# Output projections with both memory parts first, and two k-blocks of the gate ahead of the first head's odd scores

## The chip, the cores and the metric

One Trainium2 chip, one core of it. The time is the device time in microseconds of one execution. Three runs of the kernel before gave 2028.35, 2029.74 and 2031.55 us; the median is 2029.74 us.

## The reference, cut to what matters

The kernel computes a decoder trunk of two layers on a sequence of 512 tokens with 1024 channels. Layer 0 mixes with gated linear attention (GLA), layer 1 with a convolution module. In both, four memory heads attend to 256 memory rows, and one output projection takes the mixer's result `y` (1024 rows of the weight) and the memory heads' result `m` (512 rows) together.

```python
for i in range(2):
    x = layer_norm(ALPHA * x + 0.5 * swiglu(x, ffn1_w_gu[i], ffn1_w_down[i]), ...)
    if i == 0:
        y, qm = gla_mix(x @ gla_w_in, gla_w_gate2, gla_b_gate, gla_g_onorm)   # 4 heads, chunks of 64
        w_out = gla_w_out                                                     # (1024 + 512, 1024)
    else:
        y, qm = conv_mix(x @ conv_w_in, conv_w_dw, ...)
        w_out = conv_w_out                                                    # (1024 + 512, 1024)
    m = mem_attention(qm, mem, mem_w_kv[i])                                   # softmax over 256 rows
    x = layer_norm(ALPHA * x + concatenate([y, m]) @ w_out, ...)              # the projection changed here
    x = layer_norm(ALPHA * x + 0.5 * swiglu(x, ffn2_w_gu[i], ffn2_w_down[i]), ...)
```

In `gla_mix` the scores inside a chunk are `where(causal, qe @ ke^T, 0)`, and the result is multiplied by `silu(r)`, where `r` is a projection of `x` (the gate's projection below).

## The kernel before, in words

Activations are held with the channel on the partitions: eight blocks of 128 channels, each 128 x 512 (tokens). Every f32 product is made of three matmuls on rounded halves: high weight by high input, high weight by low input, low weight by high input (`mm3`, lines 1868 to 1870, for 512 tokens; `mm3_half`, lines 1879 to 1881, for one half of 256 tokens). ScalarE rounds a weight block to its high half (`whi`, line 715), VectorE (line 1180) or GpSimd (`lo_blocks`, line 539) makes the low half (`wlo`); `lo_ready` counts finished low halves. The order on each engine is written out by hand, engine by engine, and engines meet only at semaphores. TensorE runs its instructions in the order of its block.

**The output projection** works on pairs of output blocks: pairs 0 and 1 (blocks 0 to 3) for all 512 tokens, and the last two pairs (blocks 4 to 7) for each half of the tokens in turn. `out_a` (line 2123) multiplies the memory part, 4 k-blocks (`A_K`), `out_b` (line 2133) the mixer's part, 8 k-blocks (`B_K`), into the banks `OUT_BANKS`: pair 0 uses banks 0 and 1, pair 1 banks 2 and 3. `out_halves` (line 2150) then does blocks 4 to 7 and uses banks 0, 1 for its p = 0 and banks 2, 3 for its p = 1. For one half and one p, the memory part is 24 matmuls of 256 columns, the mixer's part (B) 48. The memory part's weights lie in a spare buffer (`a_spare`; its low halves are made by GpSimd in `spare_lo_parts`).

VectorE takes the banks away in `residual_out` (line 1427): `residual_pair` scales the layer's input (`scaled_x`, lines 1312 to 1317), adds the bank (line 1335, which increments `y_evac`), adds to the running sum (line 1291 or 1288) and to the running sum of squares (line 1299), whose squares ScalarE makes (line 779). Between pair 0 and pair 1 it makes the low half of one weight block (`split_lo(n0 + 6, 0)`, line 1180). The halves are taken away by `half_block` (line 1356), and after the first half the layer norm's sums are taken (`sums` on TensorE, lines 1929 and 1938). `y_evac` at `Y_BASE + 2` says that banks 0 and 1 are free again, at `Y_BASE + 4` that banks 2 and 3 are.

**The gated linear attention** runs head by head. `keys_and_att(h)` (line 2390) transposes the keys (line 2396), makes the scores of even sub-chunks (line 2402) in bank 5 and of odd ones (line 2408, "odd scores") in bank 6. Banks 6 and 7 held the transposed probabilities of the memory attention, which ScalarE (line 915) and VectorE (line 1568) copy out; so for head 0 the odd scores wait for `pt_evac`. `gates_of_r(first, count)` (line 2332) is the gate's projection, one k-block for two output blocks at a time (6 matmuls of 512 columns); its pieces are spread among the attention's steps. `outputs(0, 3)` (line 2210) makes the memory output of the fourth memory head. VectorE's `mask_att(0)` (line 1692) reads the scores when `att_mm` is incremented, and `state_sums` (line 2418) waits for it.

Of the kernel before, what the change touches and what calls it, by code (L numbers as in the profile page):

```python
# [102 lines left out]
def before(counts):  # L103
    return [sum(counts[:i]) for i in range(len(counts))]


Y_BASE = before(HALVED)
# [10 lines left out]
def half_no(ln, h, d):  # L118
    return HALF_BASE[ln] + (DK - HALVED[ln]) * h + d - HALVED[ln]
# [33 lines left out]
def build(nc, a, out):  # L153
# [3 lines left out]
    with ExitStack() as ctx:  # L157
        def sem(name):
            return ctx.enter_context(nc.semaphore(name))
# [9 lines left out]
        def sb(name, shape, dt=F32):  # L169
# [41 lines left out]
            ("ex0_hi", [P, 3, 4, P], F32R), ("ex0_lo", [P, 3, 4, P], F32R),  # L211
            ("t_hi", [P, 4, 4, HALF], F32R), ("t_lo", [P, 4, 4, HALF], F32R), ("hid", [P, FK, SEQ], F32))
        *_, s12_1 = views(("h_hi_7", [P, FK, SEQ], F32R), ("h_7", [P, FK - 2, SEQ], F32), ("s12_1", [P, 2, 4, P], F32))
        *_, p5_copy = views(("h_hi_8", [P, FK, SEQ], F32R), ("h_8", [P, FK, SEQ], F32), ("p5_copy", [P, HALF], F32))
        qkv, mo_hi_g, mo_lo_g, qm_g, bk, ke, v_tok = views(
# [57 lines left out]
        def a_spare(ln):  # L273

            return a_spare_g if ln == LN_GLA_OUT else a_spare_c

        def mean_at(ln):
# [9 lines left out]
        hi_ready, lo_ready, w_used = sem("hi_ready"), sem("lo_ready"), sem("w_used")  # L287
# [6 lines left out]
        y_even, y_evac, res_done, u0_ready, u_acc, q_acc, sq_done = (  # L294
            sem(n) for n in ("y_even", "y_evac", "res_done", "u0_ready", "u_acc", "q_acc", "sq_done"))
# [1568 lines left out]
        def _(pe):  # L1864
# [7 lines left out]
            def mm3(to, s, k, t, hi, lo, start, stop):  # L1872

                return mm3_of(to, whi[:, s], wlo[:, s], k, t, hi, lo, start, stop)

            def mm3_half(h, to, w_hi, w_lo, k, t, hi, lo, k_in, start, stop):

                w, tok = slice(t * P, t * P + P), slice(HALF * h, HALF * h + HALF)
                nc.tensor.matmul(to[:, tok], w_hi[:, k, w], hi[:, k_in, tok], start=start, stop=False, skip_group_check=True)  # L1879
                nc.tensor.matmul(to[:, tok], w_hi[:, k, w], lo[:, k_in, tok], start=False, stop=False, skip_group_check=True)  # L1880
                return nc.tensor.matmul(to[:, tok], w_lo[:, k, w], hi[:, k_in, tok], start=False, stop=stop,  # L1881
                                        skip_group_check=True)
# [38 lines left out]
            def sums(ln, h, spread=True):  # L1921

                tok, bs, no = tokens(ln, h), blocks(ln, h), half_no(ln, h, DK - 1) + 1
                if HALVED[ln] == DK:
                    pe.wait_ge(u_acc, ACC_BASE[ln] + DK - 1)
                else:
                    pe.wait_ge(u_half, no)
                if spread:
                    nc.tensor.matmul(mean_at(ln), ones[:, :], usum[:, tok], start=True, stop=True,
                                     skip_group_check=True).then_inc(mean_mm, 1)  # L1930
                for j, x in enumerate((usum, qsum)):
                    if j and HALVED[ln] == DK:
                        pe.wait_ge(q_acc, ACC_BASE[ln] + DK - 1)
                    elif j:
                        pe.wait_ge(q_half, no)
                    for b in bs:
                        c = 2 * bs[0] + len(bs) * j + b - bs[0]
                        last = nc.tensor.matmul(bank[5][:, c:c + 1], x[:, b * P:(b + 1) * P], ones[:, 0:1],
                                                start=(HALVED[ln] == DK and c == 0), stop=(j == 1 and b == bs[-1]),
                                                skip_group_check=True)  # L1940
                last.then_inc(stats_mm, 1)

            def spread_rstd(ln, h):

                tok = tokens(ln, h)
                pe.wait_ge(rstd_diag, UNIT[ln] + h + 1)
                nc.tensor.matmul(bank[7][:, tok], ones[:, :], diag_rstd[:, tok], start=True, stop=True,
                                 skip_group_check=True).then_inc(rstd_mm, 1)
# [201 lines left out]
            def out_halves(ln, n0, mo_hi, mo_lo, y_h, y_l):  # L2150

                spare = a_spare(ln)
                for h in range(2):
                    for p in range(2):
                        def memory_part(t):
                            for k in range(A_K):
                                mm3_half(h, bank[OUT_BANKS[2][h][2 * p + t]], spare[:, 0, A_K * p:A_K * p + A_K],
                                         spare[:, 1, A_K * p:A_K * p + A_K], k, t, mo_hi, mo_lo, k, h == 0 and k == 0, False)

                        if h == 0:  # L2160
                            pe.wait_ge(lo_ready, n0 + 5 + p)
                            pe.wait_ge(y_evac, Y_BASE[ln] + 2 * p + 2)
                            memory_part(0)
                            memory_part(1)
                            pe.wait_ge(lo_ready, n0 + 7 + p)
                        else:
                            pe.wait_ge(y_half, half_no(ln, 0, 5 + 2 * p) + 1)
                        for t in range(2):
                            to = bank[OUT_BANKS[2][h][2 * p + t]]
                            if h:  # L2170
                                memory_part(t)
                            for k in range(B_K):
                                last = mm3_half(h, to, whi[:, p], wlo[:, p], k, t, y_h, y_l, k, False, k == B_K - 1)
                            if h == 0 or t == 0:
                                last.then_inc(y_even, 1)
                            else:
                                last.then_inc(w_used, 1 if p else 3)
                            if h == 1 and p == 0:
                                if t == 0:
                                    sums(ln, 0)  # L2180
                                else:
                                    spread_rstd(ln, 0)
# [123 lines left out]
            n0 = GLA_N  # L2306
# [25 lines left out]
            def gates_of_r(first, count):  # L2332

                for i in range(first, first + count):
                    j, k = divmod(i, DK)
                    if k == 0:
                        pe.wait_ge(lo_ready, n0 + 12 + j + 1)
                        if j < 3:
                            pe.wait_ge(gla_evac, 21 + 2 * j)
                        else:  # L2340
                            pe.wait_ge(o_read, 16)
                    for t in range(2):
                        last = mm3(bank[R_BANK[j][t]][:, :], j % 2, k, t, xhi[:, k, :], xlo[:, k, :], k == 0, k == DK - 1)
                    if k == DK - 1:
                        last.then_inc(w_used, 1)
# [44 lines left out]
            def keys_and_att(h):  # L2390
                pe.wait_ge(prods, 4 * h + 4)
                pe.wait_ge(q_block, 2 * h + 2)
                if h:
                    pe.wait_ge(kdt_evac, h)
                for b in range(TB):
                    last = nc.tensor.transpose(bank[4][:, b * P:(b + 1) * P], qkv[:, 4 + h, b * P:(b + 1) * P], ident[:, :])
                last.then_inc(kdt_mm, 1)
                if h:
                    pe.wait_ge(att_evac, 2 * h)
                for b in range(TB):  # L2400
                    tok = slice(b * P, (b + 1) * P)
                    nc.tensor.matmul(bank[5][:, tok], ke[:, h, tok], qkv[:, h, tok], start=True, stop=True)
                if h:
                    pe.wait_ge(state_done, (TB - 1) * (h - 1) + 1)
                else:
                    pe.wait_ge(pt_evac, 2 * HEADS)
                for b in range(TB):
                    last = nc.tensor.matmul(bank[6][:, HALF + b * CHUNK:HALF + (b + 1) * CHUNK], ke[:, h, b * P:(b + 1) * P],
                                            q_odd[:, h, b, :], start=True, stop=True)
                last.then_inc(att_mm, 1)  # L2410

            def state_sums(h):
# [7 lines left out]
                last.then_inc(ds_mm, 1)  # L2420

            keys_and_att(0)
            gates_of_r(0, 2)
            outputs(0, 3)
            gates_of_r(2, 2)
            pe.wait_ge(mo_done, 4)
# [44 lines left out]
            n0 = CONV_N  # L2471
# [61 lines left out]
            ln = LN_FFN[3]  # L2533
# [59 lines left out]
```

## Time and profile before

| what | value |
|---|---|
| median of three runs | 2029.74 us |
| the profiled execution | 2030.78 us |
| its span, first to last instruction | 2028.9 us |
| TensorE busy | 2009.3 us, 99% |
| VectorE busy | 1349.0 us, 66% |
| ScalarE busy | 810.9 us, 40% |
| GpSimd busy | 816.9 us, 40% |
| mean granted clock of TensorE | 0.997 of full speed |

Times in the rows are microseconds from the span's start. PE is TensorE, DVE VectorE, ACT ScalarE, POOL GpSimd. A matmul's duration in the timeline includes its way through the array, so consecutive starts tell the pace: 256-column matmuls start 0.12 us apart, 512-column ones 0.23 us apart. "[1.82 <-DVE u L1335]" behind a row says that the engine was idle 1.82 us before it, and which instruction ended the idle time.

### The profile page before, as it was taken

How to read it: one execution, taken by the hardware profiler on the slowest of the kernel's cores; microseconds unless marked ns; L12 is line 12 of the kernel's file. 1: busy time of each engine (PE TensorE's matmuls, PEld its weight loads, DVE VectorE, ACT ScalarE, POOL GpSimd, SP SyncE). 2: the span in 40 equal slices, each digit the busy share in tenths (PEclk: the TensorE clock that was granted, in tenths of full speed). 3: DMA queues.
4: the chain of work that ended last, by engine and by line, in shares of the span. 5: the costliest groups of instructions: out<-in, count | busy, mean ns of one | idle time of the engine just before them, and what ended most of it. 6: DMA issues, size and time to landing. Idle time of an engine off the chain costs nothing.

```text
span 2028.9 us, 33888 instructions
## 1 busy us (share of the span) xinstructions
PE 2009.3 (99%) x13253; PEld 1841.2 (91%) x13253; DVE 1349.0 (66%) x1851; ACT 810.9 (40%) x1165; POOL 816.9 (40%) x575
## 2 busy tenths in 40 slices
PE   9999999999999999999999999999999999999998
PEld 9899998888988999999899999889887799999887
DVE  4477774553425768887466777646899986777645
ACT  5433352263433354444234444423353435433422
POOL 1588830044423458880015888001100435887000
PEclk9999999999999999999999999999999999999999
DMA  7533332332212235453232545323544322332232
GB/s 253 208 125 124 124 130 97 107 106 63 84 32 73 94 104 163 147 165 107 93 103 94 166 145 168 103 96 101 185 125 177 99 89 84 104 103 93 90 102 89
DMA packets 229511, 239.10 MB, mean 118 GB/s; under 512 B 5999, under 2 KB 222189, under 8 KB 227628
## 3 DMA queue, kind: packets, MB, share of 16 engines
q1 hardware_dynamic: 228780, 235.68, 35.4%
q10 hardware_dynamic: 640, 2.16, 0.3%
q8 instruction: 62, 1.02, 0.2%
q14 instruction: 29, 0.24, 0.0%
HBM read 215.80 MB, written 22.02 MB: 117 GB/s over the span
## 4 chain that ended last, share of the span: by engine, by line
PE 89%; DVE 3%; POOL 3%; ACT 2%; issue 2%; DMA 1%; DVEq 0%; SPq 0%; ACTq 0%; POOLq 0%
PE bank L1868 12%; PE bank L1869 12%; PE bank L1870 12%; PE bank L2004 11%; PE bank L2006 11%; PE bank L2005 11%; PE bank L1879 3%; PE bank L1880 3%; PE bank L1881 3%; PE bank L1958 1%; ACT whi L715 1%; DVE wlo L1180 1%; PE bank L1963 1%; PE bank L2327 1%; PE bank L2328 1%
## 5 line engine op out<-in xcount | busy, mean ns | idle before, releaser
L715 ACT CAST whi<-raw 128x2048 fp32r<-128x2048 f32 (+3 forms) x190 | 322.3, 1696 | 869.5 <-POOL scratch L599 433.9
L1180 DVE TENSOR_TENSOR wlo<-raw,whi 128x2048 fp32r<-128x2048 f32 (+2 forms) x164 | 355.1, 2165 | 232.8 <-ACT whi L715 232.6
L576 POOL TENSOR_TENSOR tiny<-tiny 128x2 f32<-128x2 f32 (+1 forms) x13 | 9.4, 725 | 567.1 <-DVE tiny L1460 567.1
L539 POOL TENSOR_TENSOR wlo<-raw,whi 128x256 fp32r<-128x256 f32 x128 | 100.2, 818 | 304.1 <-DVE wlo L1180 177.0
L595 POOL TENSOR_TENSOR raw<-raw 128x512 f32<-128x512 f32 x72 | 219.2, 3045 | 0.0
L1868 PE MATMUL bank<-h_hi,whi 128*128 128x512 f32 x528 | 207.1, 392 | 0.0
L1869 PE MATMUL bank<-h_lo,whi 128*128 128x512 f32 x528 | 205.5, 389 | 0.0
L1870 PE MATMUL bank<-h_hi,wlo 128*128 128x512 f32 x528 | 205.5, 389 | 0.0
L599 POOL TENSOR_TENSOR scratch<-raw,s 128x512 f32<-128x512 f32 x72 | 152.8, 2122 | 51.2 <-DVE ex_lo L1187 51.2
L2004 PE MATMUL bank<-t_hi,whi 128*128 128x256 f32 x576 | 163.7, 284 | 1.6 <-DVE bank L1247 1.6
L2004 PE MATMUL bank<-t_hi,ex_hi 128*128 128x256 f32 x576 | 163.8, 284 | 0.9 <-DVE bank L1239 0.4
L2005 PE MATMUL bank<-xlo,whi 128*128 128x256 f32 x576 | 163.1, 283 | 0.0
L2006 PE MATMUL bank<-xhi,wlo 128*128 128x256 f32 x576 | 163.1, 283 | 0.0
L2004 PE MATMUL bank<-xhi,whi 128*128 128x256 f32 x576 | 163.0, 283 | 0.0
L2005 PE MATMUL bank<-t_lo,whi 128*128 128x256 f32 x576 | 163.0, 283 | 0.0
L2006 PE MATMUL bank<-t_hi,wlo 128*128 128x256 f32 x576 | 163.0, 283 | 0.0
L2005 PE MATMUL bank<-t_lo,ex_hi 128*128 128x256 f32 x576 | 163.0, 283 | 0.0
L2006 PE MATMUL bank<-t_hi,ex_lo 128*128 128x256 f32 x576 | 163.0, 283 | 0.0
L1868 PE MATMUL bank<-xhi,whi 128*128 128x512 f32 x400 | 160.8, 402 | 0.0
L1869 PE MATMUL bank<-xlo,whi 128*128 128x512 f32 x400 | 157.2, 393 | 0.0
L1870 PE MATMUL bank<-xhi,wlo 128*128 128x512 f32 x400 | 157.0, 392 | 0.0
L592 POOL TENSOR_TENSOR s<-raw 128x512 f32<-128x512 f32 x72 | 97.4, 1353 | 128.4 <-DMA raw<-in_ffn_w_gu_dram 72.9
(376 smaller groups left out, 5808.5 us busy)
## 6 DMA issues: line engine op xcount, KB each, us to landing
raw<-in_ffn_w_gu_dram SPq DMA_DIRECT2D x88, 1024.0 KB, 4.9
raw<-in_ffn_w_down_dram SPq DMA_DIRECT2D x32, 896.0 KB, 4.6
raw<-in_ffn_w_down_dram SPq DMA_DIRECT2D x32, 512.0 KB, 3.4
raw<-in_gla_w_in_dram SPq DMA_DIRECT2D x14, 1024.0 KB, 5.0
early_raw<-in_conv_w_in_dram SPq DMA_DIRECT2D x18, 512.0 KB, 4.2
lo_scratch<-early_lo SPq DMA_DIRECT2D x18, 512.0 KB, 3.2
diag_scratch<-diag_tmp SPq DMA_DIRECT2D x8, 1024.0 KB, 7.9
raw<-in_conv_w_in_dram SPq DMA_DIRECT2D x16, 512.0 KB, 5.0
```

The lines of the kernel that those rows point to most:

```text
L539: last = nc.gpsimd.tensor_tensor(to[:, k, :], whole[:, k, :], high[:, k, :].bitcast(F32), ALU.subtract)
L592: nc.gpsimd.tensor_tensor(s12[s][:, 0], a21, a22, ALU.add).then_inc(w_sum, 1)
L595: nc.gpsimd.tensor_tensor(a21, a21, a11, ALU.add).then_inc(w_sum, 1)
L599: nc.gpsimd.tensor_tensor(s4, a12, s12[s][:, 1], ALU.add).then_inc(w_sum, 1)
L715: nc.scalar.copy(whi[:, s, 0:kc, 0:width], raw[:, s, 0:kc, 0:width]).then_inc(hi_ready, 1)
L1180: nc.vector.tensor_tensor(wlo[:, s, 0:kc, 0:width], raw[:, s, 0:kc, 0:width], whi[:, s, 0:kc, 0:width].bitcast(F32), ALU.subtract).then_in ...
L1868: nc.tensor.matmul(to, w_hi[:, k, w], hi, start=start, stop=False)
L1869: nc.tensor.matmul(to, w_hi[:, k, w], lo, start=False, stop=False)
L1870: return nc.tensor.matmul(to, w_lo[:, k, w], hi, start=False, stop=stop)
L2004: nc.tensor.matmul(to, w_hi[:, k], hi[:, k], start=(start and k == 0), stop=False, skip_group_check=True)
L2005: nc.tensor.matmul(to, w_hi[:, k], lo[:, k], start=False, stop=False, skip_group_check=True)
L2006: last = nc.tensor.matmul(to, w_lo[:, k], hi[:, k], start=False, stop=(k == 3), skip_group_check=True)
```

## The change

In `out_halves`, in the first token half, TensorE now does the memory parts of p = 0 and of p = 1 one after the other, each behind its own two waits, and then the mixer's parts (B) of p = 0 and p = 1. Before, it did memory and B of p = 0, then memory and B of p = 1. The second token half keeps its order. This holds for both layers' projections. In the GLA attention, the first two k-blocks of the gate's projection, which followed `keys_and_att(0)`, are now issued inside it, ahead of the wait for `pt_evac` and of the odd scores of head 0. No matmul is added or removed.

```diff
--- before.py
+++ after.py
@@ -2152,23 +2152,24 @@
                 spare = a_spare(ln)
                 for h in range(2):
                     for p in range(2):
-                        def memory_part(t):
+                        def memory_part(p, t):
                             for k in range(A_K):
                                 mm3_half(h, bank[OUT_BANKS[2][h][2 * p + t]], spare[:, 0, A_K * p:A_K * p + A_K],
                                          spare[:, 1, A_K * p:A_K * p + A_K], k, t, mo_hi, mo_lo, k, h == 0 and k == 0, False)
 
                         if h == 0:
-                            pe.wait_ge(lo_ready, n0 + 5 + p)
-                            pe.wait_ge(y_evac, Y_BASE[ln] + 2 * p + 2)
-                            memory_part(0)
-                            memory_part(1)
+                            for ahead in range(2 if p == 0 else 0):
+                                pe.wait_ge(lo_ready, n0 + 5 + ahead)
+                                pe.wait_ge(y_evac, Y_BASE[ln] + 2 * ahead + 2)
+                                memory_part(ahead, 0)
+                                memory_part(ahead, 1)
                             pe.wait_ge(lo_ready, n0 + 7 + p)
                         else:
                             pe.wait_ge(y_half, half_no(ln, 0, 5 + 2 * p) + 1)
                         for t in range(2):
                             to = bank[OUT_BANKS[2][h][2 * p + t]]
                             if h:
-                                memory_part(t)
+                                memory_part(p, t)
                             for k in range(B_K):
                                 last = mm3_half(h, to, whi[:, p], wlo[:, p], k, t, y_h, y_l, k, False, k == B_K - 1)
                             if h == 0 or t == 0:
@@ -2403,6 +2404,7 @@
                 if h:
                     pe.wait_ge(state_done, (TB - 1) * (h - 1) + 1)
                 else:
+                    gates_of_r(0, 2)
                     pe.wait_ge(pt_evac, 2 * HEADS)
                 for b in range(TB):
                     last = nc.tensor.matmul(bank[6][:, HALF + b * CHUNK:HALF + (b + 1) * CHUNK], ke[:, h, b * P:(b + 1) * P],
@@ -2420,7 +2422,6 @@
                 last.then_inc(ds_mm, 1)
 
             keys_and_att(0)
-            gates_of_r(0, 2)
             outputs(0, 3)
             gates_of_r(2, 2)
             pe.wait_ge(mo_done, 4)
```

## Rows read from the trace of the kernel before

**Rows 1.** The page, part 1: busy us (share of the span) x instructions.

```profile
PE 2009.3 (99%) x13253; PEld 1841.2 (91%) x13253; DVE 1349.0 (66%) x1851; ACT 810.9 (40%) x1165; POOL 816.9 (40%) x575
```

**Rows 2.** Waits of TensorE over the whole span: line <- released by: us in total, times, longest us.

```profile
PE bank L1879 <- DVE u L1335: 3.0, 2, 1.8
...
PE bank L2408 <- ACT u L915: 1.2, 1, 1.2
```

**Rows 3.** Timeline of TensorE, GLA projection: start us, us, engine, line, out<-in, forms, [idle].

```profile
671.77 0.32 PE L1879 MATMUL bank<-y_hi,whi 128*128 128x256 f32 x1
...
677.45 0.28 PE L1881 MATMUL bank<-y_hi,wlo 128*128 128x256 f32 x1
679.55 0.36 PE L1879 MATMUL bank<-mo_hi_g,a_spare_g 128*128 128x256 f32 x1 [1.82 <-DVE u L1335]
```

**Rows 4.** Timeline of VectorE in the same stretch.

```profile
669.37 2.29 DVE L1180 TENSOR_TENSOR wlo<-raw,whi 128x2048 fp32r<-128x2048 f32 x1
...
677.58 1.10 DVE L1317 SCALAR_TENSOR_TENSOR u<-xhi,u 128x512 f32<-128x512 f32 x1
678.71 0.69 DVE L1335 SCALAR_TENSOR_TENSOR u<-bank,u 128x512 f32<-128x512 f32 x1
```

**Rows 5.** Timeline of GpSimd in the same stretch.

```profile
656.49 7.60 POOL L539 TENSOR_TENSOR a_spare_g<-raw,a_spare_g 128x256 fp32r<-128x256 f32 x8
```

**Rows 6.** Timeline of TensorE, conv projection.

```profile
1628.12 0.28 PE L1879 MATMUL bank<-c_hi,whi 128*128 128x256 f32 x1
...
1633.76 0.28 PE L1881 MATMUL bank<-c_hi,wlo 128*128 128x256 f32 x1
1635.20 0.36 PE L1879 MATMUL bank<-mo_hi_c,a_spare_c 128*128 128x256 f32 x1 [1.16 <-DVE u L1335]
```

**Rows 7.** Timeline of VectorE, conv projection.

```profile
1634.37 0.69 DVE L1335 SCALAR_TENSOR_TENSOR u<-bank,u 128x512 f32<-128x512 f32 x1
```

**Rows 8.** Timeline of GpSimd, conv projection.

```profile
1616.24 3.25 POOL L539 TENSOR_TENSOR a_spare_c<-raw,a_spare_c 128x256 fp32r<-128x256 f32 x4 [0.49 <-ACT a_spare_c L828]
```

**Rows 9.** Timeline of all engines behind the first half, GLA projection.

```profile
690.59 0.88 DVE L1373 TENSOR_TENSOR scratch<-scratch 128x256 f32<-128x256 f32 x2
...
692.58 0.59 PE L1929 MATMUL bank<-scratch,ones 128*128 128x256 f32 x2
```

**Rows 10.** Timeline of TensorE around its slow stretch.

```profile
615.76 3.63 PE L2453 MATMUL bank<-ones,ke 128*128 128x1 f32 x32
...
621.57 0.63 PE L1870 MATMUL bank<-xhi,wlo 128*128 128x512 f32 x1
622.00 0.63 PE L1868 MATMUL bank<-xhi,whi 128*128 128x512 f32 x1
```

**Rows 11.** Timeline of TensorE around the first head's scores.

```profile
553.29 1.06 PE L2402 MATMUL bank<-qkv,ke 128*128 128x128 f32 x8
555.59 1.10 PE L2408 MATMUL bank<-q_odd,ke 128*128 128x64 f32 x8 [1.24 <-ACT u L915]
556.51 0.48 PE L1868 MATMUL bank<-xhi,whi 128*128 128x512 f32 x1
...
559.36 1.88 PE L2216 MATMUL bank<-u 128*128 128x512 f32 x4
```

**Rows 12.** Stretches of 10 us, all engines: us, busy (x instructions), PEclk, DMA share, GB/s.

```profile
440.00:450.00 10.00, 10.00 (x29) 5.85 (x28) 5.52 (x6) 8.00 (x9) 4.35 (x7) 0.83 0.63 207
...
620.00:630.00 10.00, 10.00 (x34) 7.33 (x34) 7.11 (x8) 0.43 (x1) 6.70 (x5) 0.83 0.20 67
```

**Rows 13.** Timeline of TensorE, the start.

```profile
1.07 4.63 PE L2224 MATMUL bank<-ones 128*128 128x128 f32 x20 [1.07 <-POOL ones L607]
```

**Rows 14.** Timeline of GpSimd and ScalarE before the first head's scores.

```profile
544.33 1.44 POOL L539 TENSOR_TENSOR wlo<-raw,whi 128x256 fp32r<-128x256 f32 x2
...
552.18 1.07 ACT L1015 COPY v_tok<-bank 128x512 f32<-128x512 f32 x2 [3.26 <-PE bank L2328]
...
554.94 0.60 ACT L915 COPY u<-bank 128x512 f32<-128x512 f32 x1
```

## The prediction

> **What bounds the kernel now.** I read the page's busy shares first: TensorE is busy for 2009.3 of 2028.9 us [rows 1], so only two things can move the time, idle time of TensorE and the clock it is granted. I then read the list of waits of TensorE, whose twelve entries sum to about 11 us. The change touches two of them: 3.0 us in two waits of line 1879 for the DVE eviction of line 1335, and 1.2 us in one wait of line 2408 for a ScalarE copy [rows 2]. If both disappeared at no price the gain would be 4.2 us, so what matters is whether they disappear or are moved. The timelines of TensorE and of VectorE around the three places answer that. "Same" below means within 0.2%, about 4 us, which is what a measurement of this kernel can tell from no change.
>
> **Part 1, the memory parts of both pairs lead in the first half.** Nothing is added or removed: the same 24 matmuls of a pair's memory part are issued, and the same waits. Their order is changed. Before: memory of pair 0, projection (B) of pair 0, wait for `y_evac` +4, memory of pair 1, B of pair 1. After: memory of pair 0, wait for `y_evac` +4, memory of pair 1, B of pair 0, B of pair 1. So the wait for the fourth eviction moves ahead of the 48 matmuls that stood between it and the end of pair 0's memory part. Queued behind it on TensorE are now these 48 matmuls, which need nothing from the evictions of banks 2 and 3; before, they ran during the wait.
>
> In the GLA layer B of pair 0 starts at 671.77, its last matmul at 677.45, and pair 1's memory part starts at 679.55 after 1.82 us idle [rows 3]. The eviction it waits for starts at 678.71 and lasts 0.69 us, so it ends at 679.40 [rows 4]. Does anything in VectorE's way to 679.40 depend on B of pair 0? No. In order stand the low half of a weight block from 669.37 (2.29 us), scaled inputs, the third eviction, sums and squares, scaled inputs again (the last at 677.58, 1.10 us) and the fourth eviction [rows 4]. VectorE runs these without a break; they read banks that `out_b` had finished before pair 0's memory part began. The other wait in front of pair 1's memory part, for the low half of its weights, is met: GpSimd's eight blocks end at 656.49 + 7.60 = 664.1 [rows 5]. So TensorE will reach the wait at 671.77 and stand until about 679.55: 7.8 us idle in place of 1.8. The price is the work that leaves the shadow: 48 matmuls from 671.77 to one step after 677.45. A step is (677.45 - 671.77)/47 = 0.121 us, so they end at 677.57 and last **5.80 us**.
>
> In the conv layer the same rows stand at 1628.12, 1633.76 and 1635.20 (idle 1.16) [rows 6], and the eviction at 1634.37 + 0.69 = 1635.06 [rows 7]. The low halves of the spare weights end at 1616.24 + 3.25 = 1619.5 [rows 8]. TensorE will stand from 1628.12 to 1635.20, 7.1 us. Price: 1633.88 - 1628.12 = **5.76 us**. Together **+11.56 us**.
>
> Is it given back later? Behind the first half, TensorE's sums over all blocks are the next place that waits for VectorE. They start at 692.58 and VectorE's last half squares end at 690.59 + 0.88 = 691.47 [rows 9]. There is 1.1 us of slack now and no stall to save, and the later order gives VectorE more room, not less. After it, statistics, normalization and the first chunk of the next layer all start from these sums and so move with TensorE. I take 0 given back, at most the few tenths that the sums' other waits hold.
>
> **The clock after so long an idle.** Before, no idle of TensorE is longer than 1.82 us [rows 2], so no row shows a stall of 7 us. The nearest rows on both sides are these. After the 1.82 us nothing slows: the matmuls go on at 0.12 us [rows 3]. But after 32 matmuls of one column, 3.63 us [rows 10], a slow stretch follows: 512-wide matmuls start every 0.43 us (621.57 to 622.00) [rows 10] against 0.23 us in the regular stretch (2.85 us for 12) [rows 11]. The granted clock of that 10 us stretch is 0.83, and there is a second one at 440 to 450, also 0.83 [rows 12]. A mean of 0.83 with one of two levels, 2.4 and 1.2 GHz, means 0.17 x 10 x 2 = 3.4 us at 1.2 GHz. And the kernel's very first 20 matmuls of 128 columns take 4.63 us, 0.23 each [rows 13], where eight such take 1.06, 0.13 each, later [rows 11]: after no work at all some 4.6 us went slowly, whatever clock the profile notes for it. A complete idle of 7 us is nearer to these than to 1.8 us, so I take a fall to 1.2 GHz at both places. Price: a 256-wide matmul at the slow level is put at 0.43/2 = 0.213 us instead of 0.121, so 3.4 us at the low level holds 16 of them, each 0.09 late: 1.5 us. By the start's 4.6 us it is 2.0 us. I take **1.6 us** each, **+3.2 us**, near the slow stretches that have a clock row. Bounds: 0 (no fall), and 3.0 us each (a stretch twice as long).
>
> The Trainium skill's page "TensorE: Matmul & The Clock Gate", section "Loop structure matters more than you think", gives as the bad case a TensorE left idle for 8 us between matmuls, whose clock then drops to half rate. No run here shows such an idle yet; by that rule both stalls bring the fall, by the 1.82 us row alone neither would, and the sum would be 3.2 us lower.
>
> **Part 2, two k-blocks of the gate's projection before the first head's odd scores.** Before, 8 attention matmuls start at 553.29 and take 0.89 us of issue (1.06 with the last one's tail), so the odd scores could start at 554.18. They start at 555.59 [rows 11], because the copy of the fourth head's probabilities starts at 554.94 and takes 0.60 us [rows 14]. That is a stall of 1.41 us, of which the list counts 1.24. After, the 12 gate matmuls (556.51 to 559.36 before, 2.85 us) run from 554.18 to about 557.0, by when the copy has been over for 1.5 us. Their own waits are met: the low half of their weights was made by GpSimd by 544.33 + 1.44 = 545.8, and the last evictions of the value chunk end at 552.18 + 1.07 = 553.25 [rows 14]. The odd scores come 1.4 us later than before on the clock, but their reader, the mask on VectorE, stands behind the low half of the memory outputs, which waits for `outputs(0, 3)`; that comes 1.41 us sooner as the matmuls before it are the same in number. Gain **1.41 us**, bounds 1.2 and 1.5 (a few tenths of VectorE's chain may show behind it).
>
> **Sum.** 5.80 + 5.76 + 3.2 - 1.41 = **+13.35 us**. The profiled execution took 2030.78 us with a span of 2028.9; it becomes 2044.1. It lies 1.04 us above the median of the runs, so the median becomes 2029.74 + 13.35 = **2043.1 us**.
>
> **Rivals.**
> (a) The clock stays at 2.4 GHz. For it: none of the idles before brought a fall. Against it: much shorter sparse work did. Then +10.15: **2039.9**. Chance 0.12.
> (b) The other side: the fourth eviction is ready sooner. It decides at 671.77 and 1628.12: if the eviction were over by then, both waits vanish, the 3.0 us and the 1.41 us are gained, and the time is 2029.74 - 4.4 = **2025.3**. VectorE would have to be 7.6 us faster between 669.37 and 679.40, that is, do 10.0 us of work in 2.4. What speaks for it is only that its operations there last 1.1 to 1.2 us next to GpSimd's work and 0.69 elsewhere [rows 4], worth 2 to 3 us, and GpSimd's work is not moved. Chance 0.03.
> (c) The reorder does not do what it says to the wait, because the wait's row is put down to the wrong releaser and something earlier lets pair 1 start. Then only part 2 remains and part of the stall: 2029.74 - 1.41 = **2028.3**. Against it: start and eviction's end lie 0.15 us apart at both places. Chance 0.02.
> (d) The slow level lasts longer than any row of before shows, or the shifted work pulls another slow stretch in: 2 x 3.0 instead of 3.2, **2045.9**. Chance 0.10.
> The forecast has 0.73.
>
> **Numbers.** 2043.1 us. The range takes in (a) and (d) with the half microsecond by which the medians scatter: 2039.5 to 2046.5. Faster by over 0.2%: 0.03; within 0.2%: 0.02; slower: 0.95.
>
> **What would show it.** In the changed kernel the list of waits should have line 1879 waiting for line 1335 for about 14.9 us in two waits (7.8 and 7.1), and no wait of line 2408 near 555. Right after both idles the matmuls of line 1879 should start about 0.21 us apart, with a granted clock near 0.5 for some 3.4 us. VectorE's chain to the fourth eviction should be unchanged against the end of `out_b`. The prediction is wrong if the fourth eviction moves earlier than the end of pair 0's memory part, if a later wait shrinks by microseconds, or if the stretch after the idle runs at 0.12 us.

## The result and the profile after

The changed kernel takes 2045.9 us in the median of six runs (2044.02 to 2047.31), the kernel before 2030.03 us in six (2028.35 to 2031.55). The ratio is 1.0073 with a 95% interval of 1.0063 to 1.0083, that is 14.8 us slower, 12.8 to 16.8. By the medians alone it is 15.9 us. Forecast were 2043.1 us within 2039.5 to 2046.5.

The page's busy shares after, with the mean granted clock at 0.992 where it was 0.997:

```profile
PE 2015.7 (99%) x13253; PEld 1846.9 (90%) x13253; DVE 1355.8 (66%) x1851; ACT 811.7 (40%) x1165; POOL 820.9 (40%) x575
```

TensorE's waits over the whole span (line <- released by: us in total, times, longest). They answer [rows 2]: the wait of line 1879 grew from 3.0 to 13.9 us, that of line 2408 (now 2410) is gone.

```profile
PE bank L1879 <- DVE u L1335: 13.9, 2, 7.6
```

TensorE in the GLA projection, answering [rows 3] (start, duration, line, operands, idle before):

```profile
671.83 0.28 PE L1881 MATMUL bank<-mo_hi_g,a_spare_g 128*128 128x256 f32 x1
679.68 0.55 PE L1879 MATMUL bank<-mo_hi_g,a_spare_g 128*128 128x256 f32 x1 [7.58 <-DVE u L1335]
...
684.52 0.41 PE L1880 MATMUL bank<-mo_lo_g,a_spare_g 128*128 128x256 f32 x1
684.73 0.41 PE L1881 MATMUL bank<-mo_hi_g,a_spare_g 128*128 128x256 f32 x1
...
685.66 0.28 PE L1880 MATMUL bank<-y_lo,whi 128*128 128x256 f32 x1
685.78 0.28 PE L1881 MATMUL bank<-y_hi,wlo 128*128 128x256 f32 x1
```

VectorE in the same stretch, answering [rows 4]:

```profile
669.59 2.29 DVE L1180 TENSOR_TENSOR wlo<-raw,whi 128x2048 fp32r<-128x2048 f32 x1
...
677.72 1.09 DVE L1317 SCALAR_TENSOR_TENSOR u<-xhi,u 128x512 f32<-128x512 f32 x1
678.85 0.69 DVE L1335 SCALAR_TENSOR_TENSOR u<-bank,u 128x512 f32<-128x512 f32 x1
```

Pair 0's memory part ends at 671.95, one step behind 671.83, and the fourth eviction ends at 678.85 + 0.69 = 679.54. VectorE did the same things at the same times as before, within 0.25 us. TensorE stood between, 7.58 us by the list. Behind the stall the matmuls start 0.21 us apart (684.52 to 684.73), and from 685.55 on 0.12 again. The granted clock, in stretches of 1 us (us; busy of PE, PEld, DVE, ACT, POOL; PEclk, DMA share, GB/s):

```profile
674.00:675.00 1.00, 0.00 (x0) 0.00 (x0) 0.97 (x2) 0.63 (x1) 1.00 (x3) 1.00 1.08 382
675.00:676.00 1.00, 0.00 (x0) 0.00 (x0) 1.00 (x2) 0.00 (x0) 1.00 (x2) 0.62 1.02 358
...
680.00:681.00 1.00, 1.00 (x6) 1.00 (x6) 1.00 (x2) 0.20 (x1) 0.09 (x1) 0.50 0.00 0
...
684.00:685.00 1.00, 1.00 (x7) 1.00 (x6) 0.00 (x0) 0.00 (x0) 0.00 (x0) 0.50 0.57 196
685.00:686.00 1.00, 1.00 (x8) 1.00 (x8) 0.00 (x0) 0.00 (x0) 0.00 (x0) 0.76 0.00 0
```

It falls to half, 1.2 GHz, in the fourth microsecond of the idle time, and comes back 5.8 us after the matmuls resumed (0.76 in the stretch from 685 is half speed until 685.48). The conv projection repeats it (TensorE, then VectorE, then the clock), answering [rows 6, 7]:

```profile
1636.78 0.28 PE L1881 MATMUL bank<-mo_hi_c,a_spare_c 128*128 128x256 f32 x1
1643.40 0.55 PE L1879 MATMUL bank<-mo_hi_c,a_spare_c 128*128 128x256 f32 x1 [6.35 <-DVE u L1335]
```

```profile
1642.56 0.69 DVE L1335 SCALAR_TENSOR_TENSOR u<-bank,u 128x512 f32<-128x512 f32 x1
```

```profile
1640.00:1641.00 1.00, 0.00 (x0) 0.00 (x0) 1.00 (x2) 0.00 (x0) 1.00 (x2) 1.00 0.18 63
1641.00:1642.00 1.00, 0.00 (x0) 0.00 (x0) 0.96 (x2) 0.00 (x0) 1.00 (x2) 0.60 0.01 3
...
1647.00:1648.00 1.00, 1.00 (x6) 1.00 (x6) 0.60 (x1) 0.00 (x0) 0.00 (x0) 0.50 1.08 384
1648.00:1649.00 1.00, 1.00 (x11) 1.00 (x10) 0.00 (x0) 0.00 (x0) 0.00 (x0) 0.98 0.30 102
```

The attention's scores, answering [rows 11], and the stretch of the one-column matmuls, answering [rows 10]:

```profile
553.49 1.06 PE L2403 MATMUL bank<-qkv,ke 128*128 128x128 f32 x8
554.30 0.48 PE L1868 MATMUL bank<-xhi,whi 128*128 128x512 f32 x1
...
557.13 1.00 PE L2410 MATMUL bank<-q_odd,ke 128*128 128x64 f32 x8
557.97 1.94 PE L2217 MATMUL bank<-u 128*128 128x512 f32 x4
```

```profile
614.41 4.25 PE L2454 MATMUL bank<-ones,ke 128*128 128x1 f32 x32
...
626.64 1.88 PE L2461 MATMUL bank<-ke,ones 128*128 128x512 f32 x4
```

**A ledger of the 15.8 us.** Comparing the start of the same matmuls in the two profiled executions shows where the difference of the spans, 2044.7 - 2028.9, arises:

| matmuls | before | after | difference | step |
|---|---|---|---|---|
| transposes ahead of the scores | 551.98 | 552.18 | +0.20 | not of the change |
| `outputs(0, 3)` | 559.36 | 557.97 | -1.39 | **-1.59** part 2 |
| one-column matmuls | 615.76 | 614.41 | -1.35 | |
| the broadcast behind them | 626.46 | 626.64 | +0.18 | **+1.53** |
| pair 1's memory part, GLA | 679.55 | 679.68 | +0.13 | |
| the sums behind the first half, GLA | 692.58 | 701.01 | +8.43 | **+8.30** part 1 |
| pair 1's memory part, conv | 1635.20 | 1643.40 | +8.20 | |
| the sums behind the first half, conv | 1648.23 | 1664.23 | +16.00 | **+7.80** part 1 |

The two steps of part 1 are 5.80 and 5.76 us of matmuls that left the shadow (they used to run while TensorE would have waited anyway), and 2.50 and 2.04 us that remain and are put to the slower clock; the filled version below tests that. Remainders of 0.05 to 0.23 us between the rows have no named cause. Part 2's gain is there at 558 and gone at 626. Whether that last loss belongs to the change is a question for the experiments.

### The profile page after: what moved, and what is told of

The parts are those of the page before. It is cut to its first block, busy times and chain, and to the rows that moved or that the text cites. A ratio compares the mean times of both kernels' runs of the same rounds, so it can differ in the third digit from the quotient of the medians.

```text
span 2044.7 us, 33888 instructions
## 1 busy us (share of the span) xinstructions
PE 2015.7 (99%) x13253; PEld 1846.9 (90%) x13253; DVE 1355.8 (66%) x1851; ACT 811.7 (40%) x1165; POOL 820.9 (40%) x575
## 4 chain that ended last, share of the span: by engine, by line
PE 90%; DVE 3%; POOL 3%; ACT 2%; issue 2%; DMA 1%; DVEq 0%; SPq 0%; ACTq 0%; POOLq 0%
PE bank L1868 12%; PE bank L1870 12%; PE bank L1869 12%; PE bank L2004 11%; PE bank L2006 11%; PE bank L2005 11%; PE bank L1879 3%; PE bank L1880 3%; PE bank L1881 3%; PE bank L1958 1%; ACT whi L715 1%; DVE wlo L1180 1%; PE bank L1963 1%; PE bank L2329 1%; PE bank L2328 1%
```

## The experiments

The theory after the result: (1) what the order costs is the 48 matmuls that no longer run beside VectorE's way to the fourth eviction; (2) a fallen clock adds 4.5 us; (3) part 2's gain is either real or eaten by the longer slow stretch behind the one-column matmuls. The rival to (1) and (2) is that the place of the wait, or the order of the memory parts as such, makes the loss. Each time below stands beside runs of the kernel before on the same chip.

**Each part alone.** The first run has only the `out_halves` part of the change, the second only the `gates_of_r` part.

> Part 1 alone: the memory parts of both pairs lead, the gate's k-blocks stay where they were. Theory (two stalls take 11.6 us of matmuls out of the shadow, and the fallen clock after them adds 2.5 and 2.0 us): 2030.0 + 16.1 = 2046.1 us, and the stretch behind the one-column matmuls of line 2453 is as slow as before, 3.4 us at the lower clock. Rival (the clock adds nothing beyond what other places lose anyway, only the shadow counts): 2041.6 us. Second rival (part 2 keeps its 1.4 us in the changed kernel, so leaving it out costs them): 2047.3 us.

Measured: 2045.72 us (5 runs) against 2031.01 (17), ratio 1.0073, interval 1.0060 to 1.0086. All of the loss that the medians can show is in part 1. The two rivals, 2041.6 and 2047.3, lie off the median by 4.1 and 1.6 us; the first is below the lowest run (2044.29), the second is not told apart from the theory.

> Part 2 alone: the two k-blocks of the gate ahead of the odd scores, the projections as before. Theory (the 1.4 to 1.6 us gained at 555 are given back at 614 to 624, where the one-column matmuls now meet a longer stretch at the lower clock, 6.8 us in place of 3.4): 2029.5 to 2030.5 us, the same as before, and a granted clock below 1 already during the one-column matmuls. Rival (that longer slow stretch was an accident of the profiled run, the gain stays): 2028.5 us with 3.4 us of slow stretch.

Measured: 2030.25 us (11 runs) against 2031.01 (17), ratio 0.9995, interval 0.9986 to 1.0003. Part 2 alone can't be told from no change, as the theory has it, but a gain of 1.4 us (0.9993) lies in the interval too. The profiles decide more. Clock rows of the same two stretches, first of part 1 alone and then of part 2 alone:

```profile
440.00:450.00 10.00, 10.00 (x26) 5.33 (x25) 5.70 (x6) 8.03 (x9) 4.48 (x7) 0.74 0.61 202
610.00:620.00 10.00, 10.00 (x68) 9.05 (x67) 0.69 (x1) 4.20 (x7) 0.45 (x1) 1.00 0.15 52
620.00:630.00 10.00, 10.00 (x45) 7.68 (x45) 6.26 (x8) 0.00 (x0) 7.00 (x5) 1.00 0.08 23
```

```profile
440.00:450.00 10.00, 10.00 (x37) 6.07 (x35) 5.51 (x6) 7.81 (x10) 4.54 (x7) 1.00 0.61 203
610.00:620.00 10.00, 10.00 (x52) 8.90 (x51) 0.26 (x2) 2.03 (x3) 3.02 (x2) 0.76 0.01 2
620.00:630.00 10.00, 10.00 (x37) 7.45 (x37) 8.73 (x11) 1.23 (x2) 4.00 (x4) 0.90 0.32 106
```

With part 1 alone TensorE issues the same matmuls in the same order as before up to the projection at 669 us, yet the one-column matmuls are followed by no slow stretch (1.00, 1.00), where before there was one of 3.4 us [rows 12], and where the expectation had 3.4 us; at 440 it is longer instead (0.74). With part 2 alone it is 0.24 x 10 x 2 + 0.10 x 10 x 2 = 6.8 us at 1.2 GHz. From the first one-column matmul to the broadcast behind them it took 9.08 us with none, 10.70 with 3.4 us, and 12.23 and 12.25 with 6.8 us. So a slow stretch there costs 1.6 or 3.2 us, and how long it is differs between executions of the same instructions. The 1.53 us in the ledger is of this kind, and not shown to be an effect of the change. The theory's wording for this run, that the 6.8 us take the place of the 3.4, holds for the profiled execution and isn't shown as a rule; all nine profiles that bear on it are set side by side under the one-column matmuls below.

The profile of part 1 alone also shows how far the price of the clock scatters. From pair 1's memory part to the sums it takes 699.94 - 679.15 = 20.79 us in the GLA layer and 1662.80 - 1642.25 = 20.55 in the conv layer, 1.96 and 1.76 us more than before plus the shadow, against 2.50 and 2.04 with both parts.

**Is it the clock?** The changed kernel with matmuls in the two stalls (the added lines, shortened):

```diff
+    for _ in range((56 if ln == LN_GLA_OUT else 50) if ahead else 0):
+        nc.tensor.matmul(bank[6][:, 0:HALF], spare[:, 0, 0, 0:P], mo_hi[:, 0, 0:HALF], start=True, stop=True)
     pe.wait_ge(y_evac, Y_BASE[ln] + 2 * ahead + 2)
```

> The changed kernel with the two stalls filled: 56 (GLA) and 50 (conv) more matmuls of 256 columns into an unused bank stand ahead of the wait for the fourth eviction, 6.7 and 6.0 us of work whose result nobody reads. Theory (the clock's share of the loss is 4.5 us): no lower clock near 680 and 1645, 2045.9 - 4.5 = 2041.4 us. Rival (the loss is all shadow, the clock costs nothing on the path): 2045.9 us. If the added work runs past the eviction it would be later than that.

Measured: 2041.32 us (6 runs) against 2031.01 (17), ratio 1.0041, interval 1.0027 to 1.0054. The clock rows:

```profile
670.00:680.00 10.00, 9.58 (x81) 9.38 (x80) 9.79 (x10) 2.39 (x3) 8.17 (x8) 1.00 0.34 107
680.00:690.00 10.00, 10.00 (x86) 10.00 (x85) 5.95 (x13) 0.84 (x2) 0.00 (x0) 1.00 0.30 105
1640.00:1650.00 10.00, 10.00 (x84) 9.86 (x84) 6.03 (x11) 1.05 (x2) 1.50 (x2) 1.00 0.31 105
```

With TensorE kept at work the clock stays. From pair 1's memory part to the sums it now takes 697.99 - 679.18 = 18.81 us in the GLA layer and 1659.80 - 1640.98 = 18.82 in the conv layer, which is the 13.03 of before and the shadow's 5.8 with nothing left over; in the changed kernel it was 21.33 and 20.83. So the clock's 2.5 and 2.0 us are shown in place. The kernel is 4.6 us quicker than the changed one by the medians and 4.3 by the spans (2044.7 - 2040.4), against 4.5 expected; the six runs spread over 6.5 us, so that the medians come so close is partly luck.

What is left over the kernel before is 11.5 us by the spans: the shadow's 11.6, with part 2's gain taken back by the same 6.8 us at 1.2 GHz behind the one-column matmuls as in the changed kernel. By the medians it is 10.3 us, by the ratio 8.3 (5.5 to 11.0), so the times don't say whether part 2's 1.4 us are in it. Adding 106 useless matmuls makes the changed kernel faster, which no reading by the number of instructions would give.

**Does each matmul behind the wait cost its own time?** Half of pair 0's B goes back ahead of it (the edit in short, not word for word):

```diff
     for t in range(2):
         ... B of pair 0, block t ...
+        if h == 0 and p == 0 and t == 0:
+            lead(1)      # the waits and the memory part of pair 1
```

> The changed kernel with half of B of pair 0 (its first output block, 24 matmuls) put back ahead of the wait, so that only the other 24 leave the shadow. Theory (each matmul moved behind the wait costs its 0.121 us, since the eviction's time is fixed by VectorE): shadow 2 x 2.9 = 5.8 us, idle 4.8 and 4.1 us before pair 1's memory part; the clock falls less or not at all, 0 to 3 us. 2030.0 + 5.8 + (0 to 3) = 2035.8 to 2038.8 us. Rival (the place of the wait decides, not how much work stands before it): the same as the changed kernel, 2045.9 us.

Measured: 2038.47 us (5 runs) against 2031.01 (17), ratio 1.0033, interval 1.0020 to 1.0046. TensorE's waits:

```profile
PE bank L1879 <- DVE u L1335: 8.1, 2, 4.7
```

```profile
670.00:680.00 10.00, 5.33 (x29) 5.16 (x29) 9.79 (x13) 1.26 (x2) 6.25 (x7) 0.67 0.49 168
680.00:690.00 10.00, 10.00 (x84) 10.00 (x83) 6.10 (x14) 1.25 (x3) 0.00 (x0) 0.98 0.06 21
1630.00:1640.00 10.00, 6.55 (x44) 6.37 (x43) 9.78 (x12) 1.26 (x2) 6.91 (x7) 0.83 0.50 162
1640.00:1650.00 10.00, 10.00 (x86) 10.00 (x85) 6.75 (x14) 1.26 (x3) 0.00 (x0) 1.00 0.14 49
```

The waits fell from 13.9 to 8.1 us, by 5.8 us, the time of the 48 matmuls that went back. The clock still falls at both places, which stand idle for 4.67 and 3.45 us: 0.67 in the stretch from 670, 0.83 in the one from 1630. Behind the idle time 4.5 and 3.0 us are slow, for 1.9 and 1.3 us. The loss by the medians is 7.5 us, half of the changed kernel's 15.9, so the rival (the place alone decides) falls. The sum is 5.8 for the shadow, about 3 for the clock and -1.4 for part 2, as far as part 2 is worth that.

**Is the order bad, or the eviction late?** In the kernel before VectorE stands idle for 6.67 us ahead of 668.76, and only then makes the scaled inputs and evictions of blocks 2 and 3:

```profile
668.76 0.69 DVE L1296 TENSOR_TENSOR scratch<-scratch 128x512 f32<-128x512 f32 x1 [6.67 <-ACT scratch L779]
```

```profile
665.77 1.91 ACT L715 CAST whi<-raw 128x2048 fp32r<-128x2048 f32 x1 [5.16 <-DMA raw<-in_gla_w_out_dram]
667.59 1.15 ACT L779 ACTIVATE scratch<-u 128x512 f32<-128x512 f32 x2
```

It waits for ScalarE's squares of blocks 0 and 1. Their input was there from 660.79 on, but ahead of them in ScalarE's order stands a cast that started only when its weights had come, after 5.16 us of idle. So a transfer that has nothing to do with the evictions holds them up, through two engines' orders; this is read from the trace and the order of the instructions, and no run takes the transfer away. In the conv layer the idle ahead of the same line is 2.19 us. This version moves evictions and scaled inputs ahead of the running squares in `residual_out` (in short, not word for word):

```diff
-residual_pair(ln, 0, ...)          # ends with add_square(1), which waits for ScalarE's squares
-split_lo(n0 + 6, 0)
-residual_pair(ln, 1, ...)
+residual_pair(ln, 0, ..., square=False)
+scaled_x(ln, 2); scaled_x(ln, 3)
+evict(2); add_sum(ln, 2)
+split_lo(n0 + 6, 0)
+evict(3); add_sum(ln, 3)
+add_square(ln, 1, 1); add_square(ln, 2, 0); add_square(ln, 3, 1)
```

> The changed kernel's TensorE order, with VectorE's order in the projections changed: the scaled inputs of blocks 2 and 3 and the third eviction move ahead of the running squares of blocks 1 and 2, into the 6.7 us in which VectorE stood idle (662 to 669), and the fourth eviction comes right behind the low half of the weight block, at about 670 to 671 (GLA) instead of 679.4. Theory (what the order costs is decided by when the fourth eviction ends against the end of pair 0's memory part, 671.8): no stall of line 1879, no fall of the clock there, about 3.0 us less than before and part 2 on top: 2026 to 2028 us. Rival (the early reading of the banks, or the squares moved behind, makes a new stall of the same size elsewhere): 2030 us or above. Rival 2 (the order itself is bad): stays at 2040 and above.

Measured, with the whole change: 2027.17 us (8 runs) against 2030.82 (25), ratio 0.9977, interval 0.9967 to 0.9988. VectorE's third and fourth eviction (line 1440 now), and the last matmul of pair 0's memory part with the first of pair 1's:

```profile
666.80 0.68 DVE L1440 SCALAR_TENSOR_TENSOR u<-bank,u 128x512 f32<-128x512 f32 x1
...
670.53 0.68 DVE L1440 SCALAR_TENSOR_TENSOR u<-bank,u 128x512 f32<-128x512 f32 x1
```

```profile
672.29 0.28 PE L1896 MATMUL bank<-mo_hi_g,a_spare_g 128*128 128x256 f32 x1
672.41 0.28 PE L1894 MATMUL bank<-mo_hi_g,a_spare_g 128*128 128x256 f32 x1
```

The fourth eviction ends at 671.21, 1.2 us ahead of the end of pair 0's memory part at 672.41, and pair 1's follows without a gap. In the conv layer 0.9 us of wait is left. The order that cost 15 us costs nothing here that could be told from zero (the next run has the old order): what made it dear was the eviction's time. How much the whole gains is less sure than the median looks. Four of the eight runs have a mean granted clock of 0.999 and take 2023.6 to 2025.3 us, the other four have 0.996 or 0.997 and take 2029.0 to 2030.0, and the median lies between, where there is no run.

> TensorE's order in the projections as in the kernel before, part 2 as in the changed kernel, and VectorE's earlier eviction of the run before this one. Theory (the order of TensorE is worth nothing either way once the eviction is early): the same as that run within 1 us, 2026 to 2028 us. Rival (the changed order is worth something of its own, because B of pair 0 then starts 2.9 us later and its weights' low half is surely there): 0.5 to 1 us above it, with a wait of line 1879 for line 1180.

Measured, with TensorE's old order in the projections: 2026.69 us (7 runs) against 2030.82, ratio 0.9972, interval 0.9961 to 0.9984. It can't be told from the run before it. The rival expected a wait for line 1180; there is one, 0.3 us in the conv layer, and one of 0.6 us in the GLA layer for GpSimd's `wlo` (line 539), where B of pair 1 now comes before its weights:

```profile
PE bank L1894 <- POOL wlo L539: 0.6, 1, 0.6
...
PE bank L1894 <- DVE wlo L1180: 0.3, 1, 0.3
```

So the rival's mechanism is real, but its size, 0.9 us, can't be told from zero in the times.

> The kernel before with VectorE's earlier eviction alone. Theory (the two stalls of line 1879 are worth their 3.0 us, part 2 some 0.8 to 1.4): 2027.8 us. Rival (part 2 is worth nothing once measured): 2026.7 us, the same as with part 2.

Measured, with the earlier eviction and nothing else: 2028.19 us (11 runs) against 2030.18 (19), ratio 0.9989, interval 0.9980 to 0.9998. The median gain is 2.0 us. Its profile has no wait for an eviction, but 1.1 us of waits for the low halves of weights in their place (0.8 for GpSimd's, 0.3 for VectorE's), so 1.9 of the 3.0 us of stall were to be had. The rival's 2026.7 is 1.5 us off, within the scatter of single runs (2026.65 to 2029.65); that part 2 is worth something is made likelier by it, not shown. Runs of equal mean clock can be compared here: at 0.997 the means are 2028.9 against 2030.7 us of before, at 0.998 2027.2 against 2028.9, so 1.8 and 1.7 us, near the 1.9 us of stall.

**The one-column matmuls.** They were spread in eights behind the four k-blocks that stood in front of them:

```diff
-gates_of_r(20, 4)
 for h in range(HEADS):
+    gates_of_r(20 + h, 1)
     pe.wait_ge(ss_done, h + 1)
```

> Part 2 alone, and the 32 one-column matmuls of line 2453 no longer stand in one piece: eight of them follow each of the four k-blocks of the gate that stood in front of all of them. Same matmuls, same number. Theory (the slow stretch behind them costs 1.6 us at 3.4 us and 3.1 at 6.8 us of lower clock): no stretch below 1.00 between 600 and 640, 2030.3 - (1.6 to 3.1) = 2027.2 to 2028.7 us. Rival (other things fill the time, the statistics come later): 2030 us.

Measured: 2028.62 us (11 runs) against 2030.82, ratio 0.9989, interval 0.9980 to 0.9999.

> The kernel before with the one-column matmuls spread in the same way and nothing else. With the run before this one it prices part 2 where the slow stretch behind the one-column matmuls can't mask it. Theory (part 2 is worth its 1.4 us of stall): 1.4 us above that run, 2029 to 2030 us. Rival (the gain is swallowed by a later wait in the attention or the projection, which VectorE or a transfer sets): equal to that run.

Measured: 2029.47 us (11 runs) against 2030.82, ratio 0.9989, interval 0.9980 to 0.9999. In both profiles 610 to 640 is at 1.00 throughout, so the slow stretch there is gone; that alone is worth 1.4 us by the medians of the second, with an interval of the ratio that reaches from 0.2 to 4.1 us. The difference of the two, 0.85 us, is part 2's worth here; the ratios are equal, so its 1.4 us are neither shown nor refuted by times.

What the profiles say of part 2: nine of them have the one-column matmuls in one piece. The six with part 2 show 6.8 us at 1.2 GHz between 610 and 630 five times (the changed kernel, part 2 alone, filled, and the two with part 2 and the earlier eviction) and none once (half way); the three without it show 3.4 us twice (before, earlier eviction alone) and none once (part 1 alone). That hints that part 2 lengthens the slow stretch and so pays its own gain back. It is no rule: a mean clock of 0.999, as in four of eight runs of the changed order with the earlier eviction, is about 4 us at 1.2 GHz in the whole span, so those runs didn't have the 6.8 us. Whether part 2 is worth its 1.4 us in the mean stays open.

The profile of the run with the spread alone shows one more fall of the clock:

```profile
677.41 0.36 PE L1879 MATMUL bank<-mo_hi_g,a_spare_g 128*128 128x256 f32 x1 [1.82 <-DVE u L1335]
```

```profile
670.00:680.00 10.00, 8.18 (x60) 8.01 (x59) 9.76 (x12) 1.27 (x2) 7.81 (x8) 0.89 0.42 135
680.00:690.00 10.00, 10.00 (x82) 10.00 (x80) 8.83 (x19) 1.67 (x4) 0.00 (x0) 0.94 0.22 77
```

Here the clock fell after the same 1.82 us of idle that left it alone in the kernel before, at 677.70, 0.3 us after the matmuls had resumed, for (0.11 + 0.06) x 10 x 2 = 3.4 us. From pair 1's memory part to the sums it took 691.92 - 677.41 = 14.51 us, against 13.03 before.

> The three things that the runs so far point to, together: VectorE's earlier eviction, the gate's k-blocks ahead of the odd scores, and the one-column matmuls spread; TensorE's order in the projections as in the kernel before. Theory (they are independent): against 2030.8 us of before, 4.1 for eviction and gate and 1.4 to 2.2 for the spread: 2024.5 to 2025.5 us. Rival (less idle upstream only moves the wait to a transfer or VectorE): 2026.7 us, as without the spread.

Measured, all three together with TensorE's old order in the projections: 2025.33 us (9 runs) against 2030.18 (19), ratio 0.9977, interval 0.9967 to 0.9987. It beats the kernel before by 4.7 us, 2.6 to 6.7, and the changed one by some 20. Its mean granted clock is 0.999. By the medians the theory's number came, but the ratio isn't below that of the version without the spread, so what the spread adds on top is not settled.

## Why the prediction was right

**The bound and the place.** Right. TensorE is the bound, and all of the loss arose in the two stretches named, at the wait of line 1879.

**The eviction doesn't move.** Right: 679.54 after against 679.40 before. This was the step that decided the sign. The half way version (5.8 us of wait back for 48 matmuls) and the earlier eviction (no stall in the same order) show it from both sides. Rival (b) named the earlier eviction as the point from which the change would gain; its 4.4 us compare with 3.6 by the medians (4.7 by the ratio, 2.4 to 6.7) when VectorE was made to meet it. What the prediction had wrong there is the way: it held that VectorE would have to do 10.0 us of work in 2.4. No speed was needed, only another order, because 6.67 us of VectorE's time ahead of that work lay idle; the prediction started its reading at 669.37 and didn't look at what stood before.

**5.80 + 5.76 us out of the shadow.** Right; in the filled version, without a fallen clock, the two stretches take 18.81 and 18.82 us against 13.03 before, 5.78 and 5.79 more. (That its median lies 10.3 us over before, next to rival (a)'s 10.15, is no proof of it: the interval is 5.5 to 11.0.) A detail was off: the conv idle was 6.5 us (1636.90 to 1643.40) and not 7.1, as TensorE came 0.6 us later against VectorE.

**The clock, 1.6 us each.** The mechanism was right, the size too small: 2.50 and 2.04 us, 4.5 in place of 3.2. The slow stretch on the path lasted 5.8 and 4.6 us where 3.4 were assumed from the stretch behind the one-column matmuls. With part 1 alone they were 2.0 and 1.8 us, 3.7 together. The kernel's start, 4.63 us [rows 13], was nearer in size, and there too TensorE had done nothing before; but the profile notes a granted clock of 1.00 there, so it isn't shown to be the same thing. The pace at the lower level, 0.213 us, was right. The bad case that the Trainium skill gives ("TensorE: Matmul & The Clock Gate", section "Loop structure matters more than you think") has 8 us of idle drop the clock to half rate, and the trace agrees with its 7.58 us. One argument was unsafe: "after the 1.82 us nothing slows" holds in the kernel before only; the run with the spread alone shows a fall behind the same idle.

**Part 2, -1.41 us.** At its place right: 1.59 us from the transposes to `outputs(0, 3)`. As a gain of the whole not shown: alone it is 0.9995 with an interval that holds both 0 and 1.4 us, and in five of six profiles a longer slow stretch takes it back. The sum took its 1.41 us as kept.

**The missing term.** The forecast lies 2.8 us under the measured median, and 2.4 under the profiled execution (2044.1 against 2046.52). In the profiled executions 1.3 us is the clock behind the stalls, and 1.5 the longer slow stretch at 617 to 624, less a few tenths, the larger step of part 2 among them. So both things of which rival (d) was made (chance 0.10) happened, and the measured median is its 2045.9 us. That is partly luck: (d) had 6.0 us for the clock behind the stalls, where 4.5 were measured, and the other 1.5 came from the second slow stretch. The forecast of 0.73 had the direction, the place and 11.56 us of the loss; that the time stayed 0.6 us inside the upper bound is owed to the range taking (d) in. The slow stretch at 617 differs from execution to execution at unchanged code, so it should have been part of the range and not of a rival. The medians contain it in some runs and not in others: the mean granted clock of single runs goes from 0.995 to 0.998 in the kernel before, and 0.001 of it is about 4 us at 1.2 GHz, or 2 us of time.

## What to carry to other kernels

Before work is reordered around a wait, ask what ends the wait and whether it depends on the work that moves: if it does not, every matmul that changes sides costs its full time, and the stall is cured where the wait ends: here by another order on VectorE. Price a stall of the tensor engine twice, once for the time and once for the slower clock behind it, and if it can't be removed fill it with matmuls into an unused bank. An idle stretch in the other engine's stream, here 6.67 us on VectorE just ahead of the late eviction, is the first place to look for the cure. Where a gain of 1 or 2 us is at stake and the clock has slow stretches that come and go, one profile is one sample: look at the granted clock of every run before a difference is explained.

## What the runs showed of the hardware

- After 7.58 and 6.35 us of idle (both parts), TensorE ran at 1.2 GHz for another 5.8 and 4.6 us of dense matmuls, at 0.213 us in place of 0.121 for 256 columns; after 4.67 and 3.45 us (half way) for another 4.5 and 3.0 us.
- 106 matmuls of 256 columns issued into the idle time kept the clock at 2.4 GHz. They were worth 2.5 and 2.0 us at the two places, and 4.6 us by the medians.
- A busy engine can lose its clock: 32 matmuls of one column, 3.63 to 4.25 us in which the profile counts TensorE as fully busy, are followed or met by 0, 3.4 or 6.8 us at 1.2 GHz in different executions.
- An idle of 1.82 us was followed by full clock in three profiles (before, part 2 alone, part 2 with the spread) and by 3.4 us at 1.2 GHz in a fourth (the spread alone).
